# Sums over partitions moved from TensorE to GpSimd in a gated-DeltaNet decoder block

## The reference, cut to what matters

```python
q = l2norm(q) * (dk ** -0.5)        # x * rsqrt(sum(x * x) + EPS), over the head's 128 dims
k = l2norm(k)
...                                 # chunked gated delta rule: an inverse (I + A)^-1 per chunk, then a scan
o = o * lax.rsqrt(jnp.mean(o * o, axis=-1, keepdims=True) + EPS) * onorm_g
o = o * jax.nn.silu(z)
y_a = o @ w_proj_a                  # all heads side by side
```

## Time and profile before

| | before |
|---|---|
| median of three runs | 1966.86 us |
| the profiled execution: its time / its span | 1964.6 / 1962.5 us |
| TensorE busy | 1897.8 us (97%) |
| VectorE busy | 1465.7 us (75%) |
| ScalarE busy | 982.6 us (50%) |
| GpSimd busy | 313.7 us (16%) |
| share of the chain that ended last: TensorE / VectorE / DMA | 84% / 5% / 5% |
| `square_sums`, L2823, records on TensorE | 28, 592 ns each at the median |

### The profile page before, as it was taken

How to read it: one execution, slowest core, us unless ns; L and a number is a source line. 1 busy time by engine, 2 the same in 40 slices (tenths; PEclk the granted TensorE clock), 3 DMA queues, 4 the chain that set the end, 5 groups by cost and what they waited for, 6 DMA issues and landing times.

```text
span 1962.5 us, 28802 instructions
## 1 busy us (share of the span) xinstructions
PE 1897.8 (97%) x9711; PEld 1573.4 (80%) x9711; DVE 1465.7 (75%) x1918; ACT 982.6 (50%) x1354; POOL 313.7 (16%) x238
## 2 busy tenths in 40 slices
PE   6999999999999999999999999988999999999996
PEld 5778888778788888888888788877888888888882
DVE  6966676686756857668568365668999999999996
ACT  5443222301453553534535343125888888887863
POOL 0332323001102101111021000001222222222210
PEclk7999999999999999999999899988999999999998
DMA  8133223687132223212322687447999999999966
GB/s 303 33 85 101 66 83 100 208 306 253 41 107 73 71 78 101 70 55 71 106 73 69 218 278 247 138 174 272 381 379 382 385 383 383 373 394 386 398 250 257
DMA packets 225500, 398.93 MB, mean 203 GB/s; under 512 B 50805, under 2 KB 163878, under 8 KB 199974
## 3 DMA queue, kind: packets, MB, share of 16 engines
q1 hardware_dynamic: 205254, 342.28, 50.1%
q10 hardware_dynamic: 10976, 39.15, 5.2%
q0 software_dynamic: 9216, 16.80, 2.2%
HBM read 356.89 MB, written 58.06 MB: 211 GB/s over the span
## 4 chain that ended last, share of the span: by engine, by line
PE 84%; DVE 5%; DMA 5%; ACT 2%; issue 2%; SPq 1%; ACTq 0%; POOL 0%; DVEq 0%; POOLq 0%
PE ps L769 24%; PE ps L3133 17%; PE ps L2744 13%; PE ps L3177 9%; PE ps L3028 4%; PE ps L2774 3%; PE ps L3119 1%; DMA so_lo<-o_lo_d 1%; PE ps L2961 1%; PE ps L2931 1%; PE ps L2836 1%; PE ps L2865 1%; PE ps L2975 1%; PE ps L3157 1%; PE ps L2964 1%
## 5 line engine op out<-in xcount | busy, mean ns | idle before, releaser
L637 DVE TENSOR_TENSOR mw_lo<-mw_raw,mw_hi 128x2048 fp32r<-128x2048 f32 x192 | 436.9, 2290 | 43.4 <-ACT mw_hi L632 43.2
L632 ACT ACTIVATE mw_hi<-mw_raw 128x2048 fp32r<-128x2048 f32 x192 | 368.2, 1919 | 115.3 <-PE ps L3133 66.1
L769 PE MATMUL ps<-h_hi,w_lo 128*128 128x512 f32 x704 | 287.5, 408 | 2.6 <-ACT mod_rows L1441 1.3
L769 PE MATMUL ps<-h_hi,w_hi 128*128 128x512 f32 x704 | 275.0, 391 | 0.0
L769 PE MATMUL ps<-h_lo,w_hi 128*128 128x512 f32 x704 | 274.4, 390 | 0.0
L3133 PE MATMUL ps<-mw_hi,xT_lo 128*128 128x512 f32 x512 | 203.7, 398 | 2.8 <-DVE xT_lo L2513 2.0
L3133 PE MATMUL ps<-mw_hi,xT_hi 128*128 128x512 f32 x512 | 200.9, 392 | 0.0
L3133 PE MATMUL ps<-mw_lo,xT_hi 128*128 128x512 f32 x512 | 200.0, 391 | 0.0
L769 PEld LDWEIGHTS ps<-h_hi,w_hi 128*128 128x128 f32 x704 | 132.1, 188 | 28.4
L769 PEld LDWEIGHTS ps<-h_hi,w_lo 128*128 128x128 f32 x704 | 132.6, 188 | 26.9 <-ACT conv_in L1448 1.8
L769 PEld LDWEIGHTS ps<-h_lo,w_hi 128*128 128x128 f32 x704 | 132.7, 188 | 22.1
(11 more groups left out here) (431 smaller groups left out, 4009.0 us busy)
## 6 DMA issues: line engine op xcount, KB each, us to landing
mw_raw<-in_w_dram SPq DMA_DIRECT2D x192, 1024.0 KB, 8.2
w_raw<-in_w_in_dram SPq DMA_DIRECT2D x44, 512.0 KB, 4.9
ada_h<-in_w_ada_dram SPq DMA_DIRECT2D x32, 512.0 KB, 6.0
pair_w<-in_w_in_dram SPq DMA_DIRECT2D x28, 512.0 KB, 4.7
y_t<-y_d SPq DMA_DIRECT2D x7, 1024.0 KB, 10.7
ada_sc<-in_w_ada_dram SPq DMA_DIRECT2D x4, 1024.0 KB, 8.7
s_d<-sc_acc ACTq DMA_DIRECT2D x8, 512.0 KB, 5.5
gate_b_d<-gate_sig ACTq DMA_DIRECT2D x8, 512.0 KB, 4.9
```

The source lines that it names most:

```text
L632: act.activation(mw_hi[off % NSPLIT][:], mw_raw[off % NRAW][:], ACT.Copy).then_inc(mw_hi_done, 1)
L637: dve.tensor_tensor(mw_lo[off % NSPLIT][:], mw_raw[off % NRAW][:], mw_hi[off % NSPLIT][:], ALU.subtract).then_inc(mw_lo_done, 1)
L769: last = pe.matmul(dst, lhs[:, s, k], rhs[:, k, cols], start=(k == 0 and part == 0), stop=(k == KD - 1 and part == 2))
```

## The change

For heads 0 to 6, the products with ones go. VectorE writes the sum of the two squares into `norm` instead of `LX`. GpSimd sums `norm` over the 128 partitions in one instruction, `partition_all_reduce`, in place, in the next head, between its additions to `decay` and its spread over X. ScalarE takes Ln and Exp of `norm` from SBUF in the next head, behind the copies into `k_bg`. VectorE multiplies o by norm and z in the next head's beginning, behind `sub_inverse` and the q convolution. `o_hi` is made between the two evacuations of z, `o_lo` ahead of the scan; the store of `o_lo` goes to the end of the SP queue's head. TensorE's wait for the norm's Ln ahead of L2865 goes, since banks 2 and 3 are no longer used for the sums. Head 0 is written out ahead of the loop on ScalarE, VectorE and GpSimd. In the last head, the loads of o stop ahead of head 6 until the late stores of head 6 have landed; they are counted in groups of three heads, three heads and one, and the filler takes both halves of heads 0 to 5 first, and head 6 after them.

```diff
@@ GpSimd
-            with pool.Fori(0, H) as h:
-
+            def head_pool(h, first):
                 pool.wait_ge(crow_in, 16 * h + 32)
...
                 pool.tensor_tensor(decay[:], decay[:], ncum[:, :, bass.ds(h, 1)].to_broadcast([P, TT, P]), ALU.add)\
                     .then_inc(decay_log, 1)
+                if not first:
+                    pool.wait_ge(squared, past(3 * h))
+                    pool.sem_inc(waits_passed, 1)
+                    pool.partition_all_reduce(norm[:], norm[:], P, bass.bass_isa.ReduceOp.add).then_inc(dims_summed, 1)
                 pool.wait_ge(base_moved, moved(h, 160))
...
+            head_pool(0, True)
+            with pool.Fori(1, H) as h:
+                head_pool(h, False)
@@ SP queue
                 inverse_rows(h)
-                if not first:
-                    store_o_lo(h)
                 cross_rows(h)
...
                 load_crow(h + 1)
+                if not first:
+                    store_o_lo(h)
...
-            store_o_lo(H - 1)
...
-            sp.wait_ge(head_out, past(48 * (H - 1)))
             for k in range(H - 1):
+                if k == 0:
+                    sp.wait_ge(head_out, past(48 * (H - 1) - 32))
+                if k == H - 2:
+                    store_o_lo(H - 1)
+                    sp.wait_ge(head_out, past(48 * (H - 1)))
                 for dst, src in ((so_hi, o_hi_d), (so_lo, o_lo_d)):
-                    sp.dma_start(dst[:, k].bitcast(F32), src[k * P:(k + 1) * P, :]).then_inc(o_in[k // 4], 16)
+                    sp.dma_start(dst[:, k].bitcast(F32), src[k * P:(k + 1) * P, :]).then_inc(o_in[k // 3], 16)
@@ ScalarE, head_act
                                    scale=hk[:, K_BG, t:t + 1]).then_inc(k_bg_done, 1)
+                if not first:
+                    act.wait_ge(dims_summed, h)
+                    act.activation(norm[:], norm[:], ACT.Ln, bias=eps_o_col[:], scale=1.0 / P).then_inc(root_done, 1)
+                    act.wait_ge(root_done, past(2 * h - 1))
+                    act.activation(norm[:], norm[:], ACT.Exp, scale=-0.5).then_inc(root_done, 1)
                 evac_conv("head", h, 0, 1, 1)
                 finish_queries(h)
...
                     evac(None, half, z_act[:, half * HALF:(half + 1) * HALF], ACT.Silu, group("head", h, 1, half))
+                    if half == 0 and not first:
+                        act.wait_ge(head_out, past(48 * h - 32))
+                        act.activation(o_hi[:], o_raw[:], ACT.Copy).then_inc(o_hi_done, 1)
+                        act.wait_ge(o_hi_done, 2 * h - 1)
+                        act.dma_start(o_hi_d[bass.ds(h * P - P, P), :], o_hi[:].bitcast(F32)).then_inc(head_out, 16)
...
+                    if t == 0 and not first:
+                        act.wait_ge(o_hi_done, 2 * h)
...
-                for half in range(2):
-                    act.wait_ge(norm_mm, past(2 * h + half + 1))
-                    act.activation(norm[:, half * HALF:(half + 1) * HALF], ps[:, 2 + half], ACT.Ln,
-                                   bias=eps_o_col[:], scale=1.0 / P).then_inc(root_done, 1)
                 key_norms(h + 1)
-                act.wait_ge(root_done, past(2 * h + 2))
-                act.activation(norm[:], norm[:], ACT.Exp, scale=-0.5).then_inc(inv_root, 1)
                 key_roots(h + 1)
@@ VectorE, head_dve
                     gates_early(h + 1)
+                if not first:
+                    dve.wait_ge(o_hi_done, 2 * h - 1)
+                    dve.tensor_tensor(o_lo[:], o_raw[:], o_hi[:], ALU.subtract).then_inc(o_hi_done, 1)
...
-                dve.tensor_tensor(LX[:], LX[:], kk_decay[:], ALU.add).then_inc(squared, 1)
+                dve.tensor_tensor(norm[:], LX[:].rearrange("p t i -> p (t i)"),
+                                  kk_decay[:].rearrange("p t i -> p (t i)"), ALU.add).then_inc(squared, 1)
...
                 key_products(h + 1)
-                dve.wait_ge(inv_root, h + 1)
+                key_scales(h + 1)
+                split_w_lo(dve, "head", h + 1, 1)
+                sub_inverse(h + 1)
+                conv_half(h + 1, 0, 0, qk[:, 0], 1, q_conv, head_tile(h, 4))
+                dve.wait_ge(root_done, past(2 * h + 2))
                 dve.wait_ge(o_copied, past(TT * h + TT))
...
-                key_scales(h + 1)
-                split_w_lo(dve, "head", h + 1, 1)
-                sub_inverse(h + 1)
-                conv_half(h + 1, 0, 0, qk[:, 0], 1, q_conv, head_tile(h, 4))
-                dve.wait_ge(o_hi_done, 2 * h + 1)
-                dve.wait_ge(o_step, past(2 * h + 2))
-                dve.tensor_tensor(o_lo[:], o_raw[:], o_hi[:], ALU.subtract).then_inc(o_hi_done, 1)
@@ TensorE
-            def square_sums(h, bank):
-
-                pe.wait_ge(o_copied, past(TT * h + TT))
-                pe.wait_ge(squared, past(3 * h + 3))
-                for half in range(2):
-                    cols = slice(half * HALF, (half + 1) * HALF)
-                    pe.matmul(ps[:, bank + half], ones[:], o_squares[:, cols], start=True, stop=True)\
-                      .then_inc(norm_mm, 1)
...
                 pe.wait_ge(silu_done, 3 * h + 2)
-                pe.wait_ge(root_done, past(2 * h))
...
                         if n < 2 * (H - 1):
-                            half, k = n // (H - 1), n % (H - 1)
+                            early = H - 2
+                            half, k = (n // early, n % early) if n < 2 * early else (n - 2 * early, early)
                             if half == 0:
-                                pe.wait_ge(o_in[k // 4], (128, 96)[k // 4])
+                                pe.wait_ge(o_in[k // 3], (96, 96, 32)[k // 3])
...
                 tile_half("head", h, 4, head_tile(h, 4), 0)
-                square_sums(h, 2)
                 key_products(h + 1)
```

More of the change, by code:

```diff
@@ L503, in decoder_block @@
         squared = sem("squared")
-        norm_mm = sem("norm_mm")
+        dims_summed = sem("dims_summed")
         root_done = sem("root_done")
-        inv_root = sem("inv_root")
         k_root = sem("k_root")
@@ L532, in decoder_block @@
         head_out = sem("head_out")
-        o_in = [sem(f"o_in{n}") for n in range(2)]
+        o_in = [sem(f"o_in{n}") for n in range(3)]
         last_summed = sem("last_summed")
@@ L599, in decoder_block @@
         block = ctx.enter_context(nc.Block())
-        ahead = [x_turned, norm_mm, squared, o_step, m_step, wo_lo_done, out_mm, x1_done, mb_done,
+        ahead = [x_turned, squared, o_step, m_step, wo_lo_done, out_mm, x1_done, mb_done,
                  q_dec_done, head_out, logits_done, h_hi_done, h_lo_done, mb_out, o_copied, x1_turned,
@@ L1500, in last_norm @@
                 act.wait_ge(bank_free, 2 + 2 * head_tile(h, 2) + 2)
+                act.wait_ge(head_out, past(48 * h))
                 act.dma_start(gate_a_d[bass.ds(h * P, P), :], gate_a[:]).then_inc(head_out, 16)
@@ L1503, in last_norm @@
                     cols = slice(half * HALF, (half + 1) * HALF)
-                    act.wait_ge(norm_mm, past(2 * h + half + 1))
+                    act.wait_ge(dims_summed, h + half + 1)
                     act.activation(norm[:, cols], ps[:, 6 + half], ACT.Ln, bias=eps_o_col[:], scale=1.0 / P)\
@@ L1509, in last_norm @@
                     act.wait_ge(root_done, past(2 * h + half + 1))
-                    act.activation(norm[:, cols], norm[:, cols], ACT.Exp, scale=-0.5).then_inc(inv_root, 1)
+                    act.activation(norm[:, cols], norm[:, cols], ACT.Exp, scale=-0.5).then_inc(root_done, 1)
                 for half in range(2):
@@ L1514, in last_norm, with head_act @@
                     act.activation(so_hi[:, H - 1, cols], o_raw[:, cols], ACT.Copy).then_inc(o_hi_done, 1)
-            def head_act(h, last):
+            def head_act(h, first, last):
                 evac_conv("head", h, 0, 0, 1)
@@ L1583, in head_act @@
                 split_w_hi(act, "head", h + 1, 1)
-                act.wait_ge(o_step, past(2 * h + 2))
-                act.activation(o_hi[:], o_raw[:], ACT.Copy).then_inc(o_hi_done, 1)
-                act.wait_ge(o_hi_done, 2 * h + 1)
-                act.dma_start(o_hi_d[bass.ds(h * P, P), :], o_hi[:].bitcast(F32)).then_inc(head_out, 16)
-            with act.Fori(0, H - 1) as h:
-                head_act(h, False)
-            head_act(H - 1, True)
+            head_act(0, True, False)
+            with act.Fori(1, H - 1) as h:
+                head_act(h, False, False)
+            head_act(H - 1, False, True)
             def merge_hi(i, last):
@@ L2157, in last_o @@
                     cols = slice(half * HALF, (half + 1) * HALF)
-                    dve.wait_ge(inv_root, h + half + 1)
+                    dve.wait_ge(root_done, past(2 * h + 2 + half + 1))
                     dve.wait_ge(o_copied, past(TT * h + TT // 2 * (half + 1)))
@@ L2172, in _, with head_dve @@
             dve.wait_ge(mb_out, past(32 * KD))
-            def head_dve(h, last):
+            def head_dve(h, first, last):
```

(14 more changed lines are left out.)

4 lines of the change are left out of this document (1 added, 3 removed).

## The result

The changed kernel takes 1954.44 us (median of six runs, 1952.47 to 1956.32). The kernel before, run on the same chip, takes 1966.23 us (six runs, 1965.41 to 1969.48). The ratio is 0.9936, with a 95% interval of 0.9926 to 0.9946. It is faster by some 12 us, where the forecast had it 14.5 us slower. 1954.4 lies inside the stated range (1950 to 2010), near its lower end; the sign is wrong.

The account below looks back on a forecast made before the run. TensorE sets the pace in heads 0 to 6, without a gap. Per head 3.4 + 0.9 - 1.7 = +2.6 us, seven times +18, last head -3.5: +14.5, so 1981 us on the median's scale; range 1950 to 2010.

Parts of the forecast that it names:

- GpSimd's start-up: Ahead of GpSimd's sum in each head: taken as 1.3 us, so the sum runs from 648.5 to 655.0.
- The wait of 3.4 us at L2886: TensorE's first product needing the inverse waits 3.4 us a head, as the sum holds VectorE's q convolution 4.4 us.
- rival C: GpSimd's sum starts 5.7 us late, at 652.9, and misses the q convolution: about level or faster, 1956 us; chance 0.17.
- Products with ones, 12.0 us: Two products removed from TensorE in seven heads, 1.72 us each head: 12.0 us off.
- The undisturbed round trip "0.2 us late": Inversion in each head, without delay by the sum: X landed at 686.7, where TensorE wants it at 686.5.
- Length of the sum, 6.5 us: GpSimd's sum over 128 partitions in each head: three passes of 2.15 us, 6.5 us.
- The far forms of B: GpSimd's sum much slower than a tree: 303 us, near 3900, chance 0.03; or an estimated 124 us, some 2640.
- The exclusion: A VectorE instruction with two SBUF inputs waits for the rest of GpSimd's sum: 4.4 us at the q convolution.
- Clock, 0.9 us a wait: Lower granted clock behind TensorE's wait in each head: 0.9 us lost (0 to 1.7).
- ScalarE, the queues, VectorE's moved products: nothing: Moved Ln, Exp, o products and the later store of o_lo, in each head: no cost or gain in time.
- The last head, -3.5 us: Regrouped loads of o shorten TensorE's wait for so_lo and its clock loss: 3.5 us gained (0 to 5.0).
- A: GpSimd's sum doesn't hold VectorE up: 10.6 us gained in the heads, 14 with the last, 1953 us; chance 0.30.

Follow-up runs that it names:

- Experiment 2: Changed kernel with the code of GpSimd's sum loaded ahead of the wait for the squares, so the sum starts early: 1978.20 us, ratio 1.0058.
- experiment 5: Changed kernel with the two products with ones put back on TensorE, their result unread, the sum on GpSimd kept: 1965.11 us, ratio 0.9993.
- experiment 4: Changed kernel with a second, useless reduction (maximum) on GpSimd behind the sum: 1969.52 us, ratio 1.0017.
- experiment 1: Changed kernel with GpSimd's sum taken out, so the output differs: 2109.81 us, ratio 1.0737; seven heads 534.38 us.
- experiment 3: Changed kernel with the code loaded early and the sum waiting for VectorE's first step of the inversion: 1986.91 us, ratio 1.0102.
- experiment 6: Changed kernel with the sum in two instructions of 512 columns: 1956.47 us, ratio 0.9948.
- experiment 9: Changed kernel with a second addition on GpSimd behind the sum, the Ln's scale divided by a further 128: 1986.19 us, ratio 1.0094.
- Experiment 7: Changed kernel with the last head's filler taking both halves of each head's o in turn, loads counted in pairs of heads: 1946.81 us, ratio 0.9906.

## Why the prediction was wrong, step by step

**The step that failed: GpSimd's start-up.** The forecast had 1.3 us, "the nearest row is a table load of 1.28 us", and so a sum from 648.5 that meets the convolution. It is 5.8 us from the recorded configuration change to the instruction, at each of the seven sums, so the sum starts at 652.98, when the convolution has ended. The wait of 3.4 us at L2886 that rested on it, seven times, isn't there: TensorE waits for X in no head. This is the mechanism of rival C, to the place: begin at 652.9, small products of `key_scales` held, level or faster. The Trainium skill states it (GPSIMD Engine Reference, "Instruction dispatch": some 6 us of code load at the first call of a freshly loaded kernel); by that rule, the trace agrees, with 5.8 us, and here it is paid at each of the seven sums, not only at the first. I had the rule and gave its case 0.17, since no row of before showed a start-up of that size. Experiment 2 is the counterpart: with the code early TensorE waits for X, and the kernel takes 1978.2 us. That C's number, 1956, lies so near to the measured 1954.4 is luck in part: it had 7.7 us of gain in the heads and 3.5 in the last one, and the runs show 12.0 and 0.7.

**Products with ones, 12.0 us:** right, 12.0 in the heads, and put back they cost 12.1 (experiment 5).

**The undisturbed round trip "0.2 us late":** wrong by 1.3 us. L2890 comes 1.1 us behind X. `pair_cross` ends at 679.23 + 1.22 = 680.45; the forecast, put on this execution (L2890 at 686.11 for its 686.5), had 681.2. The other half microsecond is in the transfers behind it: 4.6 us from there to the landing of X, where the forecast had 5.1. L2049 itself started where forecast (659.9, less the same 0.4 us, against 659.43). C's wait of 0.6 us a head came from a hold that lasts to the sum's end, 659.4. VectorE is let go at 657.4, L2049 starts with next to no delay, and with the reserve beside it a head keeps the whole 1.72 us.

**Length of the sum, 6.5 us:** 6.13. Right in size. Its reason, three passes of 2.15 us over the columns, isn't shown, and doesn't explain that a maximum over the same columns takes 3.23 us (experiment 4).

**The far forms of B:** a slip in the working. The sum of 303 us is priced by the room in GpSimd's queue (303 - 29.5, some 275 us a head). By the hold on VectorE, as for B itself, it would be 300 us a head, near 4060, and the estimate of 124 us beside it would come to some 2810 and not 2640. Nothing else rests on them.

**The exclusion:** right that it exists, shown by experiments 1, 2, 3, 6 and 9: an instruction of VectorE is longer beside the sum, and another one when the sum moves. Too strong in one way, as an instruction with two SBUF operands or a `TENSOR_SCALAR` is let go 4.4 us into the 6.13 (only a copy was held again near the end), and too weak in another, as a `TENSOR_SCALAR` with one SBUF tensor is held at all (0.49 to 3.27 us, 0.17 to 4.27). The Trainium skill (SBUF — State Buffer, "Who interferes with whom") names `tensor_scalar` among the operations that can take the shared pair, which I had passed over. `kk_decay` and `k_dec`, which read PSUM, were not held (1.28 and 2.15 us beside a running sum). The same section of the Trainium skill says that who comes first keeps the port for its whole instruction; the runs agree on the waiting, and differ on its length for all but the copy (4.4 of 6.13 us), and the measurement decides. In the changed kernel it takes 1.7 us out of a gap in which VectorE waited for `sub_raw` anyway.

**Clock, 0.9 us a wait:** too small. Against the 76.30 us busy of an undisturbed head, TensorE's busy time is 77.84 in experiment 2 (idle 1.74 us in the head) and 79.08 in experiment 3 (idle 3.31): 1.5 and 2.8 us a head for the lower clock. It doesn't go in step with the wait. The head ahead in experiment 2 lost 5.9 us behind a wait of 1.45, and in experiment 4 waits of 0.4 to 1.0 us came with 8.4 us over the heads.

**Once per head, seven times:** it is six heads that can wait.

**ScalarE, the queues, VectorE's moved products: nothing.** Right: no wait of TensorE is put down to them.

**The last head, -3.5 us:** -0.7. The forecast counted that the second group now stands behind 12 loads, not 14, and missed that it is asked for sooner. The wait in the timeline of TensorE, and the windows view of what follows (us, busy, clock), to be read beside the earlier trace rows:

```profile
1091.48 0.79 PE L768 MATMUL ps<-so_hi,w_lo 128*128 128x512 f32 x1 [4.52 <-DMA so_lo<-o_lo_d]
```

```profile
1091.50:1097.00 5.50, 5.50 (x19) 0.55 0.57 196
```

Counted from the start of the last head, TensorE asked at 31.7 us before (1104.97 - 3.29 - 1069.95) and asks at 27.7 now (1091.48 - 4.52 - 1059.25); the loads landed at 35.0 and land at 32.2. Four microseconds sooner asked, 2.8 sooner landed: the wait grows from 3.29 to 4.52 us. Of the four, 1.3 come from the first group, now three heads and no longer four (3.96 us of work, before 5.27). The other 2.7 come from a filler that starts sooner, 23.75 us into the last head where it was 26.46, above all because the granted clock in the small products ahead of it was higher. The windows view of TensorE, the same 8 us of the last head before, after and in experiment 5:

```profile
1085.95:1093.95 8.00, 7.54 (x48) 0.50 1.00 368
```

```profile
1075.25:1083.25 8.00, 7.17 (x59) 0.79 1.01 407
```

```profile
1088.08:1096.08 8.00, 7.66 (x51) 0.50 1.01 394
```

Experiment 5 has the groups of three heads and the low clock: it asks at 29.8 us and waits 1.98. Why the clock differs there is open. That the last head is shorter all the same, by 0.7 us, is the clock as well: idle time grows by 1.4 us (4.28 to 5.69), and busy time falls by 2.1 (45.73 to 43.63):

```profile
1069.95:1119.96 50.01, 45.73 (x302) 39.97 (x301) 21.55 (x35) 13.44 (x33) 3.31 (x4) 0.86 0.55 191
```

Experiment 7 takes the wait away by using both halves of a head before the next one; with that order the same loads come in time.

**What would show it.** Of the signs named, the 5 us behind `norm`, the head of 76.3 us and the unstretched L2025 told of C and A against the forecast. "If none of VectorE's instructions is longer" is the weak one: the convolution is as long as before, and beside the sum only L2135 is longer, an instruction of 0.16 us.

## What to carry to other kernels

When an instruction moves to an engine that does work of another kind around it, its start-up can decide where it lands, and so what it collides with; bound it from both sides and work out the result at both ends, rather than take the nearest row of another engine. Such a reduction on GpSimd should start when VectorE reads PSUM or waits for a transfer; an early start can be worse than a late one (here by 24 us). A forecast that comes out right in its total should be read term by term all the same: in experiment 2 a wait of half the size and a dearer clock add up to it. Where a filler waits for loads, work out both when the group lands and when it is asked for, and use what has landed fully before the next piece is needed.

## What the runs showed of the hardware

- The sum over 128 partitions, float32 in place: 6.13 us for 1024 columns, 3.25 to 3.32 for 512; the maximum 3.23 us for 1024.
- The start-up of 5.8 us stands ahead of every sum with other GpSimd work in between, and not ahead of a second one right behind the first (0.21 us, experiments 4 and 9). An explicit load ahead of the wait hides it whole (experiment 2: the sum starts 0.24 us behind `norm`).
- VectorE is held for the first 4.3 to 4.4 us of a sum of 6.13, and for the first 1.75 of a maximum of 3.23. In the last part of the sum a product of two SBUF operands runs in its usual 0.42 us, while a copy of 0.17 us takes 0.52 and is let go 0.14 us before the end (experiments 3 and 9). Why there are two holds is open. In the other direction the sum waited 1.06 us for a VectorE split that had begun 0.02 us before (7.19 us against 6.13, experiment 2).
- Waits of TensorE of 1.6 to 1.7 us in a head cost 1.5 to 1.7 us of lower clock on top, and waits of 3.2 to 3.4 us 1.9 to 3.0 (experiments 2, 3 and 9). One wait of 1.45 us cost 5.9 (experiment 2), and with six waits for X of 4.2 us in all came 8.4 (experiment 4).
